# Seven block products for two FFN weight chunks in place of eight, with the sums of the blocks made on GpSimd

## The chip, the cores and the metric

The kernel runs on one core of a Trainium2 chip. The metric is the device time of one execution in microseconds. Before the change three runs gave 2638.39, 2638.54 and 2638.65 us; the median is 2638.54 us. The engines are named as in the profile: PE is TensorE (its weight loads are PEld), DVE is VectorE, ACT is ScalarE, POOL is GpSimd, SP is the queue from which the weight loads are issued.

## The reference, cut to what matters

The model is two layers of a first block and two layers of a second block, on 256 tokens of width 1024. Each layer has an FFN, a mixer and a second FFN, so there are eight FFNs in all:

```python
def swiglu(h, w_gate, w_up, w_down):                 # first block
    return (jax.nn.silu(h @ w_gate) * (h @ w_up)) @ w_down

def swiglu_ffn(h, w_in, w_out):                      # second block
    gate, up = jnp.split(h @ w_in, 2, axis=-1)
    return (jax.nn.silu(gate) * up) @ w_out
# h: 256 x 1024, gate and up: 1024 x 2816 each, down: 2816 x 1024, all float32
```

The change touches the products `h @ w_gate` and `h @ w_up` alone; the mixers and the down product compute what they did.

## The kernel before, in words

**Three products for one.** Every float32 operand is split into a high part, rounded to the type that PE multiplies (`F32R`), and a low part, the rest. `three` (L522 to L524) issues high by high, high by low and low by high into one sum in PSUM. So each weight tile that lands in `ring` (128x1024) is first copied by ACT into `wh` (`high`, L547), and then `wl = ring - wh` is made by DVE or POOL (`low`, L555). Both buffers have four slots; a slot of `wh` is free for the next tile when PE has begun the tile behind it (`used`), and a slot of `ring` when the low part has been made.

**An FFN.** The 2816 columns of gate and of up are cut into 11 chunks of 256. One chunk is four tiles, each with two blocks of 128 rows of 256 gate and 256 up columns, 512 side by side. The activations (`xh`, `xl`, turned so that the width lies on the partitions) are the stationary operand: for each of 8 row blocks and each of 2 groups of 128 tokens (`q`) PE runs three matmuls of 512 columns. A chunk is 48 of them, a tile 12. Chunk 0 goes once through its tiles for each `q`; the others take both `q` in one pass. The sums lie in two banks of PSUM (`GU_BANKS`), ACT applies `Silu` to the gate half (L1436), DVE multiplies with the up half (`gated`, L2023), PE turns the result (four transposes, `turn`, L725), ACT and DVE split it (`turned`, L1441 and L2029). The down product reads 22 more tiles.

**What sets the order.** Each engine's instructions are written out in one fixed order; engines wait for each other with counting semaphores, and nothing is reordered. In the FFNs DVE makes all low parts and POOL none but for a few tiles at their edges; in the mixers POOL makes nearly all of them. SP issues the loads of all tiles in order, each as two transfers of 256 KB, and waits before each for the low part of the tile four before it.

The functions that the diff touches:

Of the kernel before, what the change touches and what calls it, by code (L numbers as in the profile page):

```python
# [13 lines left out]

# [59 lines left out]
assert T1 % SLOTS == 0 and T2 % SLOTS == 0  # L74
# [59 lines left out]
class Tiles:  # L134


    def __init__(self, quads, k=0, widths=None):
        self.quads, self.k, self.it, self.widths = quads, k, 0, widths or {}

    def number(self, i=0):  # L140
        return (self.quads + self.it) * SLOTS + self.k + i

    def slot(self, i=0):
        return (self.k + i) % SLOTS

# [24 lines left out]
def program(nc, a, out, plan):  # L170
# [4 lines left out]
    with ExitStack() as ctx:  # L175
# [16 lines left out]
        wh = sb("wh", [SLOTS, SLOT], F32R)  # L192
        wl = sb("wl", [SLOTS, SLOT], F32R)
# [22 lines left out]
        cmask = masks[:, 0:S]  # L216
        W = sb("W", [WIDE])
# [74 lines left out]
        rows = view(D)  # L292
# [2396 lines left out]
```

## Time and profile before

| what | value |
|---|---|
| median of three runs | 2638.54 us |
| span of the profiled execution | 2636.4 us |
| around the span (difference of the two) | 2.1 us |
| PE busy | 2616.3 us, 99% of the span |
| DVE busy | 1497.4 us, 57% |
| ACT busy | 1435.8 us, 54% |
| POOL busy | 851.6 us, 32% |
| memory traffic | mean 170 GB/s |

The profiled execution's own time is its span and the 2.1 us beside it, so it agrees with the median. Matmuls are pipelined and each is shown longer than its distance to the next, so the busy time of PE says that it never pauses and not how fast it is: its pace is read from the starts in the timeline. POOL is busy in the mixers and idle in the FFNs. An engine's record of an instruction runs from its start to its end; a time in it in which the instruction could not yet read its operands counts as busy.

### The profile page before, as it was taken

What the parts mean: (1) busy time and instruction counts of PE and PEld (TensorE: products, weight loads), DVE (VectorE), ACT (ScalarE), POOL (GpSimd) and SP (SyncE); (2) the same over time, 40 slices, a digit from 0 to 9 for tenths busy, and PEclk for the clock granted to TensorE, in tenths of its full rate; (3) what the DMA queues carried; (4) which work ended last, traced back from release to release, by engine and by line L of the source; (5) the groups of instructions that cost most, each with busy time, mean ns of one, the idle gap of its engine ahead of it and who ended that gap; (6) DMA issues with size and microseconds to landing.
All of it is one profiled execution on the core that took longest, in us unless ns stands there. A gap on an engine that the chain in (4) does not pass through costs nothing.

```text
span 2636.4 us, 45280 instructions
## 1 busy us (share of the span) xinstructions
PE 2616.3 (99%) x16746; PEld 2280.3 (86%) x16746; DVE 1497.4 (57%) x2457; ACT 1435.8 (54%) x2122; POOL 851.6 (32%) x443
## 2 busy tenths in 40 slices
PE   9999999999999999999999999999999999999999
PEld 8888998888888998888889999988888899999887
DVE  5553645545543745545556787355455567873654
ACT  5546665445445655445445645664455557456643
POOL 0007672000017675000008755810000086558100
PEclk9999999999999999999999999999999999999999
DMA  7555546655655546556557742566565587425664
GB/s 226 184 182 177 146 155 188 187 189 180 189 176 175 152 153 198 184 184 194 187 164 184 170 88 82 170 190 187 180 198 186 153 195 166 84 79 184 191 184 144
DMA packets 351973, 447.17 MB, mean 170 GB/s; under 512 B 32446, under 2 KB 241344, under 8 KB 351776
## 3 DMA queue, kind: packets, MB, share of 16 engines
q1 hardware_dynamic: 350032, 442.80, 56.8%
q8 instruction: 133, 2.18, 0.3%
q10 hardware_dynamic: 816, 1.21, 0.1%
q0 software_dynamic: 928, 0.45, 0.1%
q14 instruction: 64, 0.52, 0.1%
HBM read 443.31 MB, written 1.05 MB: 169 GB/s over the span
## 4 chain that ended last, share of the span: by engine, by line
PE 95%; ACT 3%; DVE 2%; issue 0%; POOL 0%; DVEq 0%; ACTq 0%; POOLq 0%
PE PS L522 29%; PE PS L524 29%; PE PS L523 28%; PE PS L725 1%; PE PS L1110 1%; PE PS L1183 1%; PE PS L691 1%; PE PS L1173 1%; PE PS L913 1%; DVE PS L2303 1%; PE PS L960 0%; ACT xh L1320 0%; ACT wh L547 0%; PE PS L826 0%; PE PS L1207 0%
## 5 line engine op out<-in xcount | busy, mean ns | idle before, releaser
L547 ACT ACTIVATE wh<-ring 128x1024 fp32r<-128x1024 f32 (+2 forms) x840 | 883.4, 1055 | 879.9 <-PE PS L522 857.0
L555 POOL TENSOR_TENSOR wl<-ring,wh 128x1024 fp32r<-128x1024 f32 (+2 forms) x332 | 786.1, 2384 | 1589.6 <-ACT wh L547 1589.1
L555 DVE TENSOR_TENSOR wl<-ring,wh 128x1024 fp32r<-128x1024 f32 x508 | 621.4, 1225 | 612.7 <-ACT wh L547 612.4
L522 PE MATMUL PS<-wh,xh 128*128 128x512 f32 (+2 forms) x1760 | 692.3, 393 | 1.0 <-POOL wl L555 1.0
L524 PE MATMUL PS<-wh,xl 128*128 128x512 f32 (+2 forms) x1760 | 682.5, 388 | 0.0
L523 PE MATMUL PS<-wl,xh 128*128 128x512 f32 (+2 forms) x1760 | 681.3, 387 | 0.0
L522 PE MATMUL PS<-xh,wh 128*128 128x256 f32 x1536 | 444.8, 290 | 0.1
L524 PE MATMUL PS<-xh,wl 128*128 128x256 f32 x1536 | 434.4, 283 | 0.0
L523 PE MATMUL PS<-xl,wh 128*128 128x256 f32 x1536 | 434.3, 283 | 0.0
L524 PEld LDWEIGHTS PS<-wh,xl 128*128 128x128 f32 x1760 | 330.5, 188 | 68.4
L522 PEld LDWEIGHTS PS<-wh,xh 128*128 128x128 f32 x1760 | 330.7, 188 | 68.0 <-issue 2.7
L523 PEld LDWEIGHTS PS<-wl,xh 128*128 128x128 f32 x1760 | 331.0, 188 | 63.6
L522 PEld LDWEIGHTS PS<-xh,wh 128*128 128x128 f32 x1536 | 294.1, 191 | 8.4 <-issue 3.4
L523 PEld LDWEIGHTS PS<-xl,wh 128*128 128x128 f32 x1536 | 294.4, 192 | 2.5 <-issue 2.4
L524 PEld LDWEIGHTS PS<-xh,wl 128*128 128x128 f32 x1536 | 294.3, 192 | 0.0
L522 PE MATMUL PS<-wh,hh 128*128 128x512 f32 x704 | 275.2, 391 | 0.0
L524 PE MATMUL PS<-wh,hl 128*128 128x512 f32 x704 | 274.1, 389 | 0.0
L523 PE MATMUL PS<-wl,hh 128*128 128x512 f32 x704 | 273.9, 389 | 0.0
L2303 DVE SCALAR_TENSOR_TENSOR PS<-W,cols,PS 128x256 f32<-128x256 f32 x464 | 186.8, 479 | 0.0
L524 PEld LDWEIGHTS PS<-wh,hl 128*128 128x128 f32 x704 | 132.1, 188 | 27.6
L523 PEld LDWEIGHTS PS<-wl,hh 128*128 128x128 f32 x704 | 132.2, 188 | 27.1
L522 PEld LDWEIGHTS PS<-wh,hh 128*128 128x128 f32 x704 | 132.2, 188 | 26.9
(319 smaller groups left out, 2439.0 us busy)
## 6 DMA issues: line engine op xcount, KB each, us to landing
ring<-in_ffn_w_in_dram SPq DMA_DIRECT2D x352, 256.0 KB, 3.0
ring<-in_mix_w_in_dram SPq DMA_DIRECT2D x256, 256.0 KB, 3.9
ring<-in_ffn_w_gate_dram SPq DMA_DIRECT2D x176, 256.0 KB, 2.9
ring<-in_ffn_w_up_dram SPq DMA_DIRECT2D x176, 256.0 KB, 3.1
ring<-in_ffn_w_down_dram SPq DMA_DIRECT2D x176, 256.0 KB, 2.8
ring<-in_w_in_dram SPq DMA_DIRECT2D x176, 256.0 KB, 3.0
ring<-in_ffn_w_out_dram SPq DMA_DIRECT2D x176, 256.0 KB, 2.8
ring<-in_w_branch_dram SPq DMA_DIRECT2D x32, 256.0 KB, 2.9
```

The lines of the kernel that those rows point to most:

```text
L522: first_ = mm(o, w[0], x[0], start=start, stop=False, skip_group_check=True)
L523: mm(o, w[0], x[1], start=False, stop=False, skip_group_check=True)
L524: return first_, mm(o, w[1], x[0], start=False, stop=stop, skip_group_check=True)
L547: act_(dst, src, ACT.Copy).then_inc(hi_ready, 1)
L555: (engine or v_).tensor_tensor(dst, src, part_views(t, wh)[0], ALU.subtract).then_inc(lo[t.slot()], 1)
L691: ins = nc.tensor.transpose(xt_bank(s, q, k), src[:, q, k * P:(k + 1) * P], ident[:])
L725: ins = nc.tensor.transpose(bank(4 + c % 2, o, o + P), act2[:, c % 2, q, j * P:(j + 1) * P], ident[:])
L913: ins = mm(bank((6 if j == 0 else 4) + half, o, o + nk), heads[r, qb, q * P:(q + 1) * P], heads[r, kb, 0:nk], start=True, stop=True)
L1110: ins = mm(PS[r, 3 + 2 * c, h * HD:(h + 1) * HD], src[c][r, h, :], ident[r, r], start=True, stop=True)
L1173: ins = mm(o, alc[c][r, h, :], lower(Tc[c][r, h, :], l), start=True, stop=True)
L1183: ins = mm(PS[r, 2 + 2 * c, S + h * 32:S + (h + 1) * 32], Uc[c][r, h, :], m1n[c][r, h, :], start=True, stop=True)
L2303: ins = v_.scalar_tensor_tensor(conv[:, b, :] if tap == TAPS - 1 else part, src, w, part, ALU.mult, ALU.add)
```

## The change

Three of the pairs of neighbouring chunks, (3, 4), (6, 7) and (9, 10), are multiplied as 2 by 2 block matrices. The blocks of the left side are the activations cut into front and back half of the width and into the two token groups; the blocks of the right side, `b11`, `b12`, `b21`, `b22`, are 512 rows of one chunk (front or back half of the width, first or second chunk). Seven products M1 to M7 of 4 row blocks each are formed, in place of eight, and the four results are sums of them (Winograd's form of Strassen's algorithm). A product is 12 matmuls of 512 columns and a pair 84, against 96.

- **Loads.** The blocks of a pair land in four buffers of 128x2048 (1 MB each, as two transfers of 512 KB), each loaded again once the product that reads it is done; `b12` waits for M7, `b21` for M2 and for the sum T4. The other five chunks and the down tiles still pass through `ring`. The 28 transfers of `load_params2` move from POOL's queue to SP's.
- **Sums of weights.** POOL makes for each pair T1 = b12 - b11, T2 = b22 - T1, T3 = b22 - b12 and T4 = b21 - T2, each 128x2048. For each FFN it makes once the sums of the activations, S0 (`xh + xl`, 128x2048) and S1 to S4 (128x4x128).
- **High and low parts.** ACT makes the high parts of all seven right sides, 128x2048 each, into both planes of one slot of `wp` (`wh` and `wl` of before as one buffer). DVE makes the low parts of M1, M5 and M3 whole (128x2048), those of M6 in two halves, and half of those of M7, M2 and M4; POOL makes the other halves of these three. The low parts mostly overwrite their source, so that those of M1 and M5 wait for T1 and T2.
- **Sums of products.** ACT copies three of the results out of PSUM, DVE adds three times (128x512).

```diff
+PAIRS = ((3, 4), (6, 7), (9, 10))
+PLAIN_AT = {0: 0, 1: 4, 2: 8, 5: 21, 8: 34}
+PAIR_AT = (12, 25, 38)
+SUM_OF = {"M1": 0, "M5": 1, "M6": 2, "M3": 4, "M7": 5, "M2": 6, "M4": 8}
+SUM_BANKS = {"M1": 6, "M6": 6, "M7": 6, "M4": 6, "M5": 7, "M3": 7, "M2": 3}
+RAW_OF = {"M1": "b11", "M5": "t1", "M6": "t2", "M3": "b22", "M7": "t3", "M2": "b21", "M4": "t4"}
...
+        raw = {n: view(BLOCK) for n in ("b11", "b12", "b21", "b22", "t1", "t2")}
+        low_of = {n: lows[:, i * BLOCK:(i + 1) * BLOCK] for i, n in enumerate(raw)}
+        raw["t3"], low_of["t3"] = raw["b12"], low_of["b12"]
...
+                for i, (name, product) in enumerate((("b11", "M1"), ("b22", "M3"), ("b12", "M7"), ("b21", "M2"))):
...
+                        sp.wait_ge(track_[0].sem, track_[0].at(f"{tag_}.{product}.{p_}", lay_))
+                        if name == "b21":
+                            sp.wait_ge(track_[3].sem, track_[3].at(f"{tag_}.T4.{p_}", lay_))
+                    load_block(sp, p, name, gate, up)
...
+            return (engine or v_).tensor_tensor(dst, src, highs, ALU.subtract)
...
+                product("M1", x_part(0, 0), True)
...
+                product("M5", sum_part(1, 1), True)
+                turn(PAIRS[p][0] - 1)
...
+                product("M6", sum_part(0, 0))
...
+                product("M3", sum_part(1, 0))
...
+                product("M7", sum_part(0, 1))
+                product("M2", x_part(4, 0), True)
...
+                product("M4", x_part(4, 1))
...
+            plain(1, (0,))
+            plain(2, (1,))
+            for p, (c, d) in enumerate(PAIRS):
+                two_chunks(p)
+                if p < 2:
+                    plain(d + 1, (d, c))
...
+                low_behind("M6", 0)
+                low_behind("M6", 1)
                 gated(c - 1)
-                low(e, t, 3 if c == 1 else 2)
+                low_whole(p, "M3", "T3")
                 turned(c - 1)
-                chunk(c)
-                if c < CHUNKS:
-                    low(e, t, 2)
+                low_shared(p, "M7")
+                low_behind("M2", 0)
+                summed(p, bank(7), bank(7), u2s, "M3", "u2s", "c12")
+                low_shared(p, "M4")
+                t.k += PAIR_SLOTS
+                gated_of(d, 0, bank(7, CHUNK, 2 * CHUNK))
+                summed(p, m5s, bank(6), m5s, "M7", "m5s", "c22")
+                low(e, t, 1)
+                gated_of(d, 1, m5s[:, CHUNK:2 * CHUNK])
+                summed(p, bank(3), bank(3), m1s, "M2", "m1s", "c11")
+                low(e, t, 1)
+                gated_of(c, 0, bank(3, CHUNK, 2 * CHUNK))
+                low(e, t, 1)
+                gated_of(c, 1, bank(6, CHUNK, 2 * CHUNK))
+                low(e, t, 1)
+                turned(d)
+                if p < 2:
+                    low_whole(p + 1, "M1", "T1")
...
+                turned(c)
+                if p < 2:
+                    low_whole(p + 1, "M5", "T2")
...
+            did(p_.tensor_tensor(sq, xh, xl, ALU.add), "S0")
...
+            for p in range(3):
...
+                did(p_.tensor_tensor(raw["t1"], raw["b12"], raw["b11"], ALU.subtract), f"T1.{p}")
+                own(f"T1.{p}")
+                e.wait_ge(blocks_in["b22"], landed_)
+                did(p_.tensor_tensor(raw["t2"], raw["b22"], raw["t1"], ALU.subtract), f"T2.{p}")
+                own(f"T2.{p}")
+                did(p_.tensor_tensor(raw["t3"], raw["b22"], raw["b12"], ALU.subtract), f"T3.{p}")
+                e.wait_ge(blocks_in["b21"], landed_)
+                if p == 0:
+                    e.wait_ge(ff[2].sem, ff[2].at(f"{tag}.sl1"))
+                else:
+                    e.wait_ge(ff[0].sem, ff[0].at(f"{tag}.M4.{p - 1}"))
+                did(p_.tensor_tensor(raw["t4"], raw["b21"], raw["t2"], ALU.subtract), f"T4.{p}")
+                own(f"T3.{p}")
+                low_sum(e, t, "M7", p_, 1).then_inc(lo[t.slot(SUM_OF["M7"])], 1)
+                low_sum(e, t, "M2", p_, 1).then_inc(lo[t.slot(SUM_OF["M2"] + 1)], 1)
+                own(f"T4.{p}")
+                low_sum(e, t, "M4", p_, 1).then_inc(lo[t.slot(SUM_OF["M4"])], 1)
```

The order of POOL's instructions, from the setup of the masks on. Before, the first mixer's low parts (L555) come right behind it:

```order
L2630 AFFINE_SELECT masks<-masks 128x128
L555 TENSOR_TENSOR wl<-ring,wh 128x1024 x4
L555 TENSOR_TENSOR wl<-ring,wh 128x912 x4
L555 TENSOR_TENSOR wl<-ring,wh 128x1024 x4
L555 TENSOR_TENSOR wl<-ring,wh 128x512 x4
```

After, the first FFN stands between: S0 to S4, and then for each pair T1 to T4 and three halves of low parts (`W` holds the weight blocks, `sum_lows` the same memory as the place of the low parts). The first pair is shown; the rows from L2915 on come three times.

```order
L2901 TENSOR_TENSOR sq<-xh,xl 128x2048
L2903 TENSOR_TENSOR sq<-sq 128x4x128
L2905 TENSOR_TENSOR sq<-sq 128x4x128
L2907 TENSOR_TENSOR sq<-sq 128x4x128
L2909 TENSOR_TENSOR sq<-sq 128x4x128
L2915 TENSOR_TENSOR W<-W 128x2048
L2918 TENSOR_TENSOR W<-W 128x2048
L2920 TENSOR_TENSOR W<-W 128x2048
L2926 TENSOR_TENSOR sq<-W 128x2048
L685 TENSOR_TENSOR sum_lows<-W,wp 128x1024
L685 TENSOR_TENSOR wp<-W,wp 128x1024
L685 TENSOR_TENSOR sum_low_in_squares<-sq,wp 128x1024
```

So POOL gets 26 instructions in each FFN, in which it had none but at the edges; every one reads two operands from SBUF.

The order of DVE's instructions around the change of chunk, in the first FFN before. Four low parts (L555), two `gated` (L2023) and one `turned` (L2029) are a chunk:

```order
L2029 TENSOR_TENSOR hl<-PS,hh 128x512
L555 TENSOR_TENSOR wl<-ring,wh 128x1024 x2
L2023 SCALAR_TENSOR_TENSOR act<-PS,rs,act 128x256 x2
L555 TENSOR_TENSOR wl<-ring,wh 128x1024 x2
L2029 TENSOR_TENSOR hl<-PS,hh 128x512
L555 TENSOR_TENSOR wl<-ring,wh 128x1024 x2
L2023 SCALAR_TENSOR_TENSOR act<-PS,rs,act 128x256 x2
L555 TENSOR_TENSOR wl<-ring,wh 128x1024 x2
L2029 TENSOR_TENSOR hl<-PS,hh 128x512
```

After, beside the plain chunk 5, which PE multiplies between the first pair and the second. L645 is the low part of a plain tile, L2261 is `gated`, L2289 a sum of products, L2267 is `turned`, L685 the low parts of the next pair's M1 and M5 (`W` in the second row is M5's copy with M7's bank added, `rstd` in the third holds a copy of M1):

```order
L645 TENSOR_TENSOR wp<-ring,wp 128x1024
L2261 SCALAR_TENSOR_TENSOR act<-W,rs,act 128x256
L2289 TENSOR_TENSOR PS<-PS,rstd 128x512
L645 TENSOR_TENSOR wp<-ring,wp 128x1024
L2261 SCALAR_TENSOR_TENSOR act<-PS,rs,act 128x256
L645 TENSOR_TENSOR wp<-ring,wp 128x1024
L2261 SCALAR_TENSOR_TENSOR act<-PS,rs,act 128x256
L645 TENSOR_TENSOR wp<-ring,wp 128x1024
L2267 TENSOR_TENSOR hl<-PS,hh 128x512
L685 TENSOR_TENSOR sum_lows<-W,wp 128x2048
L2267 TENSOR_TENSOR hl<-PS,hh 128x512
L685 TENSOR_TENSOR sum_lows<-W,wp 128x2048
```

The low parts of tiles stand one by one between the results of the pair before, and two whole low parts follow them. By what they wait for, POOL's T1 to T4 of the next pair belong to the same stretch.

## Rows read from the trace of the kernel before

**Rows 1.** The page: busy time of each engine, and the chain that ended last.
```profile
PE 2616.3 (99%) x16746; PEld 2280.3 (86%) x16746; DVE 1497.4 (57%) x2457; ACT 1435.8 (54%) x2122; POOL 851.6 (32%) x443
...
PE 95%; ACT 3%; DVE 2%; issue 0%; POOL 0%; DVEq 0%; ACTq 0%; POOLq 0%
```
**Rows 2.** Busy time by window, nine chunks of one FFN (columns named in its line).
```profile
core 0: us, PE busy (x) PEld busy (x) DVE busy (x) ACT busy (x) POOL busy (x), PEclk, DMA share, GB/s
25.00:149.00 124.00, 124.00 (x570) 102.62 (x569) 72.61 (x89) 62.03 (x79) 0.00 (x0) 1.00 0.61 191
```
**Rows 3.** Timeline of PE in the first FFN: start us, length us, engine, line, instruction.
```profile
10.16 0.48 PE L522 MATMUL PS<-wh,xh 128*128 128x512 f32 x1
...
24.88 0.60 PE L725 MATMUL PS<-ident,act 128*128 128x128 f32 x4
...
36.25 0.60 PE L725 MATMUL PS<-ident,act 128*128 128x128 f32 x4
...
60.81 0.39 PE L522 MATMUL PS<-wh,xh 128*128 128x512 f32 x1
...
62.85 0.39 PE L522 MATMUL PS<-wh,xh 128*128 128x512 f32 x1
```
**Rows 4.** Groups by line and shape: busy us, mean ns, then idle time before them.
```profile
L555 POOL TENSOR_TENSOR wl<-ring,wh 128x1024 fp32r<-128x1024 f32 x316 | 758.9, 2417 | 1572.6 <-ACT wh L547 1572.1
L555 POOL TENSOR_TENSOR wl<-ring,wh 128x512 fp32r<-128x512 f32 x8 | 10.2, 1294 | 6.3 <-ACT wh L547 6.3
L555 DVE TENSOR_TENSOR wl<-ring,wh 128x1024 fp32r<-128x1024 f32 x508 | 621.4, 1225 | 612.7 <-ACT wh L547 612.4
L547 ACT ACTIVATE wh<-ring 128x1024 fp32r<-128x1024 f32 x824 | 870.9, 1060 | 871.2 <-PE PS L522 848.3 <-DMA ring<-in_mix_w_in_dram 15.9 <-DMA ring<-in_w_in_dram 2.4
L1441 ACT ACTIVATE hh<-PS 128x512 fp32r<-128x512 f32 x88 | 51.1, 581 | 0.0
L2023 DVE SCALAR_TENSOR_TENSOR act<-PS,rs,act 128x256 f32<-128x256 f32 x176 | 84.2, 483 | 15.4 <-ACT act L1436 15.4
L2029 DVE TENSOR_TENSOR hl<-PS,hh 128x512 fp32r<-128x512 f32 x88 | 60.1, 683 | 0.0
```
**Rows 5.** Timeline of POOL in the first mixer.
```profile
311.34 2.39 POOL L555 TENSOR_TENSOR wl<-ring,wh 128x1024 fp32r<-128x1024 f32 x1 [0.48 <-ACT wh L547]
316.31 2.49 POOL L555 TENSOR_TENSOR wl<-ring,wh 128x1024 fp32r<-128x1024 f32 x1 [2.58 <-ACT wh L547]
319.17 2.43 POOL L555 TENSOR_TENSOR wl<-ring,wh 128x1024 fp32r<-128x1024 f32 x1 [0.37 <-ACT wh L547]
...
374.25 8.05 POOL L555 TENSOR_TENSOR wl<-ring,wh 128x1024 fp32r<-128x1024 f32 x3 [2.52 <-ACT wh L547]
```
**Rows 6.** Timeline of DVE beside rows 5.
```profile
308.28 1.22 DVE L2168 TENSOR_REDUCE W<-W 128x4 f32<-128x1024 f32 x1
...
314.37 0.42 DVE L2073 TENSOR_TENSOR W<-W,masks 128x256 f32<-128x256 f32 x1
...
316.57 2.79 DVE L2182 TENSOR_TENSOR W<-W 128x512 f32<-128x512 f32 x1
...
324.08 0.68 DVE L1932 TENSOR_TENSOR ol<-W,oh 128x512 fp32r<-128x512 f32 x1
...
376.31 3.71 DVE L1932 TENSOR_TENSOR ol<-W,oh 128x512 fp32r<-128x512 f32 x2
```
**Rows 7.** Timeline of DVE in a mixer of the second block.
```profile
1522.51 2.43 DVE L2303 SCALAR_TENSOR_TENSOR PS<-W,cols,PS 128x256 f32<-128x256 f32 x6
...
1527.59 2.00 DVE L2480 TENSOR_TENSOR W<-masks,W 128x256 f32<-128x256 f32 x1
```
**Rows 8.** Timeline of POOL beside rows 7.
```profile
1519.68 4.74 POOL L555 TENSOR_TENSOR wl<-ring,wh 128x1024 fp32r<-128x1024 f32 x2 [5.62 <-ACT wh L547]
...
1526.82 2.48 POOL L555 TENSOR_TENSOR wl<-ring,wh 128x1024 fp32r<-128x1024 f32 x1 [1.01 <-ACT wh L547]
```
**Rows 9.** The page: loads, their size and median us from issue to landing.
```profile
ring<-in_ffn_w_gate_dram SPq DMA_DIRECT2D x176, 256.0 KB, 2.9
```
**Rows 10.** Timeline of SP in the first FFN: the two transfers of a tile issued.
```profile
36.64 0.37 SPq L358 DMA_DIRECT2D ring<-in_ffn_w_gate_dram  x1
37.10 0.42 SPq L358 DMA_DIRECT2D ring<-in_ffn_w_up_dram  x1
```
**Rows 11.** Busy time by window, the first 30 us (columns as in rows 2).
```profile
0.00:30.00 30.00, 28.12 (x134) 24.12 (x135) 16.80 (x41) 20.82 (x39) 1.52 (x9) 1.00 0.82 261
```

More of the change, by code:

```diff
@@ L15 @@
+import itertools
 import math
@@ L290, in view @@
             return W[:, at:at + width]
-        rows = view(D)
+        rows = post
+        off[0] = 14656
         srow = view(P)
@@ L370, in kmajor, with ffn_number @@
             return w2d.rearrange("(k p) n -> p k n", p=P)
[L372 to L388 removed]
+        def ffn_number(s):
+            return 2 * (s // 3) + s % 3 // 2
@@ new lines, in between @@
+                    def between(last=lay == LAYERS - 1 and half == 1):
+                        if last:
+                            load_params2(sp)
+                    load_ffn(sp, t, first["ffn"], f"f{half}", lay, kmajor(a["ffn_w_gate"][lay, half]),
+                             kmajor(a["ffn_w_up"][lay, half]), a["ffn_w_down"][lay, half],
+                             (first["mix"], lay) if half == 1 else None, before, between)
+                    before = (first["ffn"], f"f{half}", lay, 2)
@@ L508, in program @@
         qd = view(512).rearrange("p (h n) -> p h n", h=4)
+        assert off[0] <= 13824, off[0]
+        off[0] = 13824
+        for c in range(QT):
+            DU["U", c] = view(512).rearrange("p (h n) -> p h n", h=4)
         wT, st = DU["T", 0], DU["T", 1]
@@ L1451, in act_ffn @@
+            silu(0)
+            high(e, t, 3)
+            turned(0)
+            chunk(1)
+            high(e, t, 2)
+            silu(1)
+            high(e, t, 1)
+            turned(1)
+            hi(0, "M1")
+            sums_high()
+            hi(0, "M5")
+            hi(0, "M6")
+            chunk(2)
+            for p, (c, d) in enumerate(PAIRS):
+                two_chunks(p, c, d)
+                for c_ in (c, d, d + 1):
+                    chunk(c_)
             tables(LN_EXP)
@@ L2039, in dve_ffn @@
+            gated(0)
+            low(e, t, 3)
+            turned(0)
+            chunk(1)
+            low(e, t, 2)
+            gated(1)
+            low(e, t, 1)
+            turned(1)
+            low_whole(0, "M1", "T1")
+            sums_low()
+            low_whole(0, "M5", "T2")
+            chunk(2)
+            for p, (c, d) in enumerate(PAIRS):
+                two_chunks(p, c, d)
+                for c_ in (c, d, d + 1):
+                    chunk(c_)
             low(e, t, 8)
```

410 lines of the change are left out of this document (297 added, 113 removed).

## The prediction

> **What bounds the kernel now.** I read first the busy times and the chain of waits: PE is busy 99% of the span, and 95% of the chain that ended last is PE [rows 1]. Then the windows: in 124 us of the first FFN PE never pauses, DVE is busy 72.61 us, ACT 62.03, POOL 0.00, and the granted clock is 1.00, the 2.4 GHz level [rows 2]. Then PE's timeline for its pace: from 60.81 to 62.85 nine matmuls of 512 columns start, 0.227 us each, so a tile of 12 takes 2.72 us; from one turn to the next (24.88 to 36.25) a chunk takes 11.37 us, that is 48 matmuls in 10.88 and 0.49 for the turn; chunk 0 takes 24.88 - 10.16 less one tile, 12.0 us [rows 3]. So an FFN's gate and up products take 12.0 + 10 x 11.37 = 125.7 us, paced by PE alone, and what PE is spared is time gained as long as the others keep up. Last I looked in the timeline of the mixers, the only places where POOL and DVE work together, at what each does to the other: that decides this case.
>
> **The term that gains.** A pair needs 84 matmuls instead of 96. With 3 pairs in each of 8 FFNs that is 288 matmuls fewer, 288 x 0.227 = 65.3 us. The turns stay.
>
> **What POOL and DVE cost each other.** In rows 5 and 6 DVE's L2182 (512 elements, both inputs in `W`) starts at 316.57, while POOL runs from 316.31 to 318.80; it ends at 319.36, 0.56 after POOL's end, and takes 2.79 us. L1932 with the same 512 elements, and with the same kinds of operands as a low part, takes 0.68 when POOL is idle. POOL's next low part, recorded from 319.17, ends at 321.60, 2.24 after DVE's end. At 376.31 two of L1932 take 3.71 us, while three POOL low parts from 374.25 take 8.05 in place of 3 x 2.39 = 7.17: POOL (to 376.64), DVE, POOL, DVE, POOL, in turn. L2480 (256 elements) ends at 1529.59, 0.29 after POOL's end at 1529.30, and takes 2.00; L2073 with as many, beside an idle POOL, takes 0.42 [rows 6 to 8]. DVE instructions with one input in SBUF are not held: six of L2303, which read `W` and PSUM, take 0.41 us each under POOL's two from 1519.68, and the reduction at 308.28 takes its 1.22 [rows 6 to 8]. So a DVE instruction with two SBUF inputs and a POOL instruction exclude each other for their whole length and take turns.
>
> The Trainium skill says the same of the cause (page "SBUF — State Buffer", section "SBUF: two separate sides"): VectorE and GpSimd share a pair of ports, held by whoever starts first for the whole instruction, and VectorE needs it for two inputs in SBUF. The trace agrees with its 0.56 and 0.29 us, and this rule speaks against this change, since it makes no exception for the low parts, which in the trace never meet POOL.
>
> In the FFNs before, nothing of this costs anything, as POOL is idle there. After, POOL has 26 instructions in every FFN, and all low parts of DVE (ring or `W`, and `wp`) have two SBUF inputs.
>
> **Prices.** POOL, 1024 elements: 2.39 alone [rows 5], 2.25 when it waited for DVE (its start is then hidden). From 512 elements at 1.29 [rows 4] the slope is 1.10 us for 512, so 2048 cost 2.39 + 2.20 = 4.6 alone, 4.45 after a wait; no row shows it, the bounds are 4.45 and 2 x 2.39 = 4.8, and I take 4.6. DVE, 1024: 1.22 alone, 1.07 after a wait (0.56 for 512 doubled, less 0.05); 2048: 2.3 and 2.13. ACT: 1.06 for 1024, 0.58 for 512 [rows 4], so 2.0 for 2048. `gated` 0.48, `turned` and a sum from PSUM 0.68 each. A block of 1 MB: 256 KB land in 2.9 us [rows 9] and the memory gave 261 GB/s at best [rows 11], 4 us for a block; with the start of a transfer I take 5, bounds 4 and 7.
>
> **One pair and the chunk beside it.** PE needs 11 x 2.72 + 3 x 0.49 = 31.4 us. The shared access is needed for POOL's T1 to T4, 4 x 4.45, and three halves, 3 x 2.25: 24.6. DVE needs it for three whole low parts 6.4, five halves and four plain tiles 9.6, and one `gated` from SBUF 0.3: 16.3. The sum is 40.9 us, 9.5 more than PE needs. Laid out in turns by the orders of both engines, T1 begins 5 us after M7 of the pair before (b12 has landed). Then DVE's low part of the first plain tile, T2, one `gated`, T3, second tile, T4, third tile follow each other without a gap: 4 x 4.45 + 3 x 1.07 + 0.3 = 21.3 us, in which PE gets two tiles and two turns, 6.4 us of work. The fourth tile, M1, M5, M6 and M3 are then DVE's alone (1.2 + 2.3 + 2.3 + 2.4 + 2.3), with 3.5 us between them for `turned`, `gated` and ACT's high part of M3, which waits for M5's start: 14.0. M7, M2 and M4 need one POOL half and one DVE half each, 3 x 3.4 = 10.2, with 1.1 before them; then 1.1 until T1. Together 21.3 + 14.0 + 1.1 + 10.2 + 1.1 = 47.7 us from T1 to T1. The engines are bound by the shared access for 41 of these and by chains through it for the rest, not by PE.
>
> **The first pair.** S0 begins some 6 us after chunk 0, when the activations' low parts are whole. S0 4.6, S1 to S4 4 x 1.3, and five low parts between them reach to 21; T1, T2, T3 with low parts of tiles 9, 10 and 11 between, 4.4 x 3 + 3.2, to 37.4. `turned`, M1's low part, the two low parts of the activations' sums (T4 waits for them) and M5's bring 45; T4 comes before M6's halves, 52; M3, and M7, M2, M4 with their shares, end at 65; M4 itself ends at 68. PE alone would end there at 12.0 + 8 x 2.72 + 2 x 0.49 + 7 x 2.72 + 0.49 = 54.3.
>
> **Sum.** Gate and up of an FFN: 68 + 2 x 47.7 + 1 (the last `gated` in front of the down product's second half) = 164.4 us, against 125.7: 38.7 more. Eight times that is 310. The profiled execution's time is its span 2636.4 and 2.1 around it, 2638.5, equal to the median; 2638.5 + 310 = 2949, and I forecast 2950. What I cost at nothing: the 28 transfers moved to SP's queue, 0.46 us from one issue to the next [rows 10], some 13 in all, which stand before chunk 5's loads of one FFN, that have 40 us; ACT's extra copies, since ACT has 7 x 2.0 + 4 x 1.06 + 3 x 0.58 + some 4 of results in 47.7 us; the bytes, which are the same as before. If ACT's cover goes, the 2 us of a high part show in M7, 48 us in all, which the range holds.
>
> **Bounds.** If the turns packed without any gap, an FFN would need the access for 9.8 (S0 to S4) + 3 x 24.6 + 16 x 1.07 + 2.1 + 3 x 12.0 = 139 us between 6 us after its start and 2.7 before its end: 147.5, 21.8 more than before, 174 in all, 2813. At the other end POOL at 4.8 instead of 4.45 adds 12 x 0.35 = 4.2 an FFN, and blocks that land in 7 us add 2 in each of two periods: 66 in all, 3015.
>
> **Rivals.**
> *They do not exclude each other here.* The low parts of DVE in FFNs never met POOL, so that it is by kinship with L1932 that I hold them back. Then POOL's 4 x 4.6 + 3 x 2.39 = 25.6 fits under PE's 31.4, DVE needs 25 or so, and the tightest chain, M6's start to M7's low part (0.58 + 2.0 + 2.39 = 5.0) fits under two products, 5.44. PE stays the bound: 2638.5 - 65.3 = 2573, up to 2600 with chains that miss. All overlaps in rows 5 to 8 speak against it. 4%. This is the only way to be faster.
> *Tight packing.* DVE gets ahead by its three tiles in stock, and gaps close: 2813 to 2870. For it speaks that four wl and wh slots are filled when T1 comes; against it that DVE's order puts results between the tiles. 16%.
> *PE's clock falls.* My layout gives PE pauses of 3 to 5 us in each stretch of T1 to T4, where before the longest stretch shown runs without one at 1.00 [rows 2]. If the clock fell to the 1.2 GHz level there and was half until the pause was over, tiles one and two stay hidden under the sums, but the third tile and the start of M1, some 2.7 us of work, would take 2.7 more in each of 24 stretches: 65 us, 3015. No row shows the clock after a pause. 20%.
> The Trainium skill ("TensorE: Matmul & The Clock Gate", part 1, "What's actually happening") has full speed as something that activity grants and idling takes away, between just these two levels; no run here shows it yet.
> *The forecast itself*, 2870 to 3000: 60%.
>
> A change within 0.2%, 5 us, could not be told from none. Faster by more: 4%. Within: 1%. Slower: 95%. The range that holds 8 in 10 reaches from 2830 to 3050.
>
> **What would show it.** PE has 16458 matmuls and its share falls to near 90%. In the chain of waits DVE and POOL have large shares in place of PE's 95%. POOL is busy 690 us more and what it waits, near 1600. The mean of a low part of a plain tile on DVE rises from 1.225 us to 2 or 3, with 5 to 6 for those that wait for a T, each ending 1.07 after POOL's instruction. A window over a middle pair and its chunk takes 47 us with PE busy 35. If the DVE rows stay at 1.2 beside a busy POOL, the whole sum is wrong, and the time is below 2600. If they are long but the kernel is far under 2813, my prices are; if windows show a clock under 1.00, the third rival adds.

## The result and the profile after

The changed kernel takes 2954.7 us, the median of four runs (2949.0 to 2957.9); the kernel before took 2638.5 beside it. The ratio is 1.120, with a 95% interval of 1.118 to 1.121: 316 us slower. The profiled execution took 2955.2 us, its span is 2953.5.

The page after: busy times, granted clock in 40 slices, and the chain that ended last, which answer to [rows 1].
```profile
span 2953.5 us, 42833 instructions
PE 2680.4 (91%) x16458; PEld 2275.9 (77%) x16458; DVE 2071.6 (70%) x2545; ACT 1608.2 (54%) x2234; POOL 1708.2 (58%) x623
PEclk9999999999999999999999999998989999999989
PE 60%; DVE 21%; issue 7%; ACT 6%; DMA 3%; POOL 2%; SPq 1%; POOLq 0%; DVEq 0%; ACTq 0%
```
PE runs 288 matmuls fewer and is no longer always busy. DVE is busy 574 us more than before, although it has only 88 instructions more, and its share of the chain has gone from 2% to 21%.

The groups by line and shape after, which answer to [rows 4]: busy us, mean ns, idle time before them.
```profile
L645 DVE TENSOR_TENSOR wp<-ring,wp 128x1024 fp32r<-128x1024 f32 x316 | 638.2, 2028 | 262.2 <-ACT wp L637 262.2
L645 POOL TENSOR_TENSOR wp<-ring,wp 128x1024 fp32r<-128x1024 f32 x316 | 758.4, 2416 | 718.7 <-ACT wp L637 718.3
L685 DVE TENSOR_TENSOR sum_lows<-W,wp 128x2048 fp32r<-128x2048 f32 x72 | 296.8, 4122 | 11.5 <-ACT wp L673 4.5 <-POOL W L2918 3.9 <-POOL W L2915 3.1
L685 DVE TENSOR_TENSOR wp<-W,wp 128x1024 fp32r<-128x1024 f32 x72 | 152.1, 2138 | 31.2 <-ACT wp L671 31.1
L2918 POOL TENSOR_TENSOR W<-W 128x2048 f32<-128x2048 f32 x24 | 132.1, 5503 | 1.9
```
The same low part of a plain tile, 1.225 us in [rows 4], now takes 2.03 in the mean. POOL's low parts in the mixers are as they were (2.42).

Where it happens: POOL and then DVE in the stretch of T1 to T4 of the second pair, in the first FFN (start us, length us).
```profile
84.16 4.62 POOL L2915 TENSOR_TENSOR W<-W 128x2048 f32<-128x2048 f32 x1 [3.15 <-DMA W<-in_ffn_w_up_dram]
88.85 5.46 POOL L2918 TENSOR_TENSOR W<-W 128x2048 f32<-128x2048 f32 x1
94.39 5.46 POOL L2920 TENSOR_TENSOR W<-W 128x2048 f32<-128x2048 f32 x1
99.79 6.63 POOL L2926 TENSOR_TENSOR sq<-W 128x2048 f32<-128x2048 f32 x1
```
```profile
84.58 5.28 DVE L645 TENSOR_TENSOR wp<-ring,wp 128x1024 fp32r<-128x1024 f32 x1
90.17 5.22 DVE L645 TENSOR_TENSOR wp<-ring,wp 128x1024 fp32r<-128x1024 f32 x1
95.92 6.08 DVE L685 TENSOR_TENSOR sum_lows<-W,wp 128x2048 fp32r<-128x2048 f32 x1
102.52 6.05 DVE L685 TENSOR_TENSOR sum_lows<-W,wp 128x2048 fp32r<-128x2048 f32 x1
```
Read the ends. T1 ends at 88.78, DVE's tile 1.08 later, at 89.86. T2 is recorded from 88.85, ends at 94.31, 4.45 after the tile; the next tile ends 1.08 after T2. So it goes through all four: one at a time, in turn.

PE in the same place, M1 and the start of M5.
```profile
98.08 0.39 PE L615 MATMUL PS<-wp,xl 128*128 128x512 f32 x1
102.05 0.51 PE L613 MATMUL PS<-wp,xh 128*128 128x512 f32 x1 [3.58 <-DVE sum_lows L685]
...
103.54 0.63 PE L614 MATMUL PS<-sum_lows,xh 128*128 128x512 f32 x1
103.97 0.63 PE L615 MATMUL PS<-wp,xl 128*128 128x512 f32 x1
...
108.62 0.50 PE L613 MATMUL PS<-wp,sums_first 128*128 128x512 f32 x1 [1.96 <-DVE sum_lows L685]
```
PE has nothing to do from 98.3 to 102.05 and starts M1 as DVE's low part ends (102.00). From the third on its matmuls start 0.43 us apart instead of 0.227: the clock has fallen to the 1.2 GHz level.

Windows of the same FFN: from the second pair's T1 to the third's; its two parts; and all gate and up products. Columns as in [rows 2].
```profile
84.16:129.17 45.01, 35.53 (x141) 26.73 (x140) 42.67 (x35) 22.27 (x24) 32.18 (x7) 0.92 0.43 133
84.16:106.50 22.34, 16.86 (x69) 12.71 (x67) 22.34 (x9) 9.35 (x11) 22.10 (x4) 0.92 0.38 121
106.50:129.17 22.67, 18.67 (x73) 14.02 (x73) 20.33 (x27) 12.92 (x13) 10.08 (x3) 0.92 0.47 146
10.20:175.40 165.20, 132.95 (x543) 101.94 (x542) 148.71 (x116) 90.49 (x114) 109.77 (x26) 0.94 0.46 150
```
In the first part DVE and POOL are both recorded as busy throughout, which two engines that take turns show, since the record counts the wait.

The loss is in the FFNs alone. From first turn to last an FFN took 113.6 us before (all eight within 113.61 to 113.65) and takes 151.2 to 154.5 after. Eight times the mean difference of 39.2 is 314 of the 316 us.

### The profile page after: what moved, and what is told of

It reads as the page before. It is cut to its first block, busy times and chain, and to the rows that moved or that the text cites. A ratio compares the mean times of both kernels' runs of the same rounds, so it can differ in the third digit from the quotient of the medians.

```text
span 2953.5 us, 42833 instructions
## 1 busy us (share of the span) xinstructions
PE 2680.4 (91%) x16458; PEld 2275.9 (77%) x16458; DVE 2071.6 (70%) x2545; ACT 1608.2 (54%) x2234; POOL 1708.2 (58%) x623
## 4 chain that ended last, share of the span: by engine, by line
PE 60%; DVE 21%; issue 7%; ACT 6%; DMA 3%; POOL 2%; SPq 1%; POOLq 0%; DVEq 0%; ACTq 0%
PE PS L613 18%; PE PS L615 17%; PE PS L614 17%; DVE wp L645 8%; DVE sum_lows L685 7%; ACT wp L673 2%; DVE wp L685 2%; DVE act L2261 1%; DMA ring<-in_ffn_w_up_dram 1%; ACT wp L637 1%; PE PS L869 1%; DMA ring<-in_ffn_w_in_dram 1%; POOL sum_low_in_squares L685 1%; DVE hl L2267 1%; ACT xh L1498 1%
## 5 line engine op out<-in xcount | busy, mean ns | idle before, releaser
L645 POOL TENSOR_TENSOR wp<-ring,wp 128x1024 fp32r<-128x1024 f32 (+2 forms) x332 | 785.6, 2383 | 735.6 <-ACT wp L637 735.2
L637 ACT ACTIVATE wp<-ring 128x1024 fp32r<-128x1024 f32 (+2 forms) x648 | 681.3, 1054 | 638.5 <-PE PS L613 535.7
L645 DVE TENSOR_TENSOR wp<-ring,wp 128x1024 fp32r<-128x1024 f32 x316 | 638.2, 2028 | 262.2 <-ACT wp L637 262.2
L613 PE MATMUL PS<-wp,xh 128*128 128x512 f32 (+2 forms) x1280 | 532.4, 416 | 118.3 <-DVE sum_lows L685 58.7
L615 PE MATMUL PS<-wp,xl 128*128 128x512 f32 (+2 forms) x1280 | 513.1, 401 | 0.0
L613 PE MATMUL PS<-xh,wp 128*128 128x256 f32 x1536 | 445.2, 290 | 0.2 <-POOL wp L645 0.2
L615 PE MATMUL PS<-xh,wp 128*128 128x256 f32 x1536 | 434.6, 283 | 0.0
L614 PE MATMUL PS<-xl,wp 128*128 128x256 f32 x1536 | 434.6, 283 | 0.0
L614 PE MATMUL PS<-wp,xh 128*128 128x512 f32 (+2 forms) x1088 | 428.7, 394 | 0.0
L613 PEld LDWEIGHTS PS<-wp,xh 128*128 128x128 f32 x1280 | 251.9, 197 | 206.4 <-DVE sum_lows L685 68.5
L613 PE MATMUL PS<-wp,hh 128*128 128x512 f32 x896 | 361.9, 404 | 9.0 <-issue 9.0
L685 DVE TENSOR_TENSOR sum_lows<-W,wp 128x2048 fp32r<-128x2048 f32 x96 | 326.2, 3398 | 29.6 <-ACT wp L673 22.6
L614 PE MATMUL PS<-wp,hh 128*128 128x512 f32 x800 | 317.8, 397 | 0.0
L613 PEld LDWEIGHTS PS<-xh,wp 128*128 128x128 f32 x1536 | 294.3, 192 | 8.7 <-issue 3.1
L615 PEld LDWEIGHTS PS<-xh,wp 128*128 128x128 f32 x1536 | 294.5, 192 | 0.0
L614 PEld LDWEIGHTS PS<-wp,xh 128*128 128x128 f32 x1088 | 210.2, 193 | 38.1
L685 POOL TENSOR_TENSOR sum_lows<-W,wp 128x1024 fp32r<-128x1024 f32 x24 | 80.9, 3372 | 213.1 <-ACT wp L673 213.1
```

Source lines behind the costliest of these rows:

```text
L613: first_ = mm(o, w[0], x[0], start=start, stop=False, skip_group_check=True)
L614: mm(o, w[0], x[1], start=False, stop=False, skip_group_check=True)
L615: return first_, mm(o, w[1], x[0], start=False, stop=stop, skip_group_check=True)
L637: act_(dst, src, ACT.Copy).then_inc(hi_ready, 1)
L645: (engine or v_).tensor_tensor(dst, src, part_views(t, wh)[0], ALU.subtract).then_inc(lo[t.slot()], 1)
L685: return (engine or v_).tensor_tensor(dst, src, highs, ALU.subtract)
```

## The experiments

All are compared with the kernel before, whose median was 2638.3 us beside them. The times are medians.

**1. POOL busy but reading nothing.** Each of T1 to T4 becomes three memsets of the same result, so the sums of weights are left out.

```diff
-                did(p_.tensor_tensor(raw["t1"], raw["b12"], raw["b11"], ALU.subtract), f"T1.{p}")
+                did(p_.memset(raw["t1"], 0.0), f"T1a.{p}")
+                own(f"T1a.{p}")
+                did(p_.memset(raw["t1"], 0.0), f"T1b.{p}")
+                own(f"T1b.{p}")
+                did(p_.memset(raw["t1"], 0.0), f"T1.{p}")
```

> Leaves out T1 to T4: each is replaced on POOL by three memsets of the same 128x2048 block, some 5.5 us together, so that POOL is busy as long as before or a little longer but reads nothing from SBUF. Theory (a POOL instruction that reads SBUF and a DVE instruction with two SBUF inputs exclude each other): DVE's low parts are no longer held by the sums, only by the three halves; the mean of a plain tile's low part on DVE falls from 2.03 us to below 1.4, and the kernel to 2600 to 2690 us. Rival one (POOL is simply too slow, and its sums come too late): POOL's time per pair is the same or longer, so 2940 us or more. Rival two (writes exclude DVE as well): the low parts stay long, 2950 to 3050 us.

Measured: 2693.5 us, ratio 1.022 (1.020 to 1.024), clock 0.992. POOL and then DVE in this kernel, from T1 of the second pair on (three memsets for each T):
```profile
71.92 1.81 POOL L2915 MEMSET W<- 128x2048 f32 x1 [1.94 <-DMA W<-in_ffn_w_up_dram]
73.79 1.82 POOL L2917 MEMSET W<- 128x2048 f32 x1
75.66 1.81 POOL L2919 MEMSET W<- 128x2048 f32 x1
```
```profile
71.98 1.21 DVE L645 TENSOR_TENSOR wp<-ring,wp 128x1024 fp32r<-128x1024 f32 x1
73.56 1.23 DVE L645 TENSOR_TENSOR wp<-ring,wp 128x1024 fp32r<-128x1024 f32 x1
78.91 2.29 DVE L685 TENSOR_TENSOR sum_lows<-W,wp 128x2048 fp32r<-128x2048 f32 x1 [1.18 <-ACT wp L673]
```
POOL is as long in its sums as before, and DVE makes its low parts at its own price, 1.22 and 2.29, through all of it. What held the low parts was that POOL read, not that it was busy or late. This takes 261 of the 316 us away. The time is 3.5 us above the expected range, and the mean of a plain tile's low part is 1.48 us, not below 1.4: S0 to S4 and the halves still read.

Other instructions of DVE are held by the memsets. In the same stretch DVE works out angles, once in the whole kernel; DVE and then POOL:
```profile
85.32 1.53 DVE L2544 CAST W<-W 128x2 f32<-128x2 int32 x1
86.89 0.17 DVE L2546 TENSOR_TENSOR W<-W 128x16 f32<-128x16 f32 x1
87.09 1.63 DVE L2547 TENSOR_SCALAR W<-W 128x16 f32<-128x16 f32 x1
```
```profile
85.02 1.81 POOL L2930 MEMSET W<- 128x2048 f32 x1
86.89 1.81 POOL L2932 MEMSET W<- 128x2048 f32 x1
```
The `CAST` and the `TENSOR_SCALAR` have one tensor as input. They end 0.02 and 0.03 us after a memset; in the changed kernel, where POOL is idle at that point, they take 0.16 and 0.17. Three more `TENSOR_SCALAR` behind them are held in the same way (1.75, 1.20 and 1.62 us), some 7 us in all. The `TENSOR_TENSOR` between, with two inputs, is not held.

**2. POOL short and reading nothing.** One memset in place of three.

```diff
-                did(p_.tensor_tensor(raw["t1"], raw["b12"], raw["b11"], ALU.subtract), f"T1.{p}")
+                did(p_.memset(raw["t1"], 0.0), f"T1.{p}")
```

> Leaves out T1 to T4: each is replaced by one memset of the block, some 1.8 us. Theory: PE is nearly the bound again; what is left are S0 to S4 and the three halves, 2590 to 2660 us, and near what the run with three memsets gives. If the sums' length were the cause, this run would be faster than the one with three memsets by 24 x 4 x 3.7 us at most, some hundred us or more.

Measured: 2683.9 us, ratio 1.018 (1.016 to 1.019). The shorter time that POOL is busy is thus worth 10 us. In the profiled executions, which are 13 us apart, 8 us of the difference lie in the first FFN, where the memsets of experiment 1 held DVE's angles, so the length of the sums is worth little by itself. The expected range was missed by 24: what is left, 111 us above the 2573 that PE's matmuls alone would give, has other causes. From one pair's M4 to the next this kernel and that of experiment 1 need 33.7 us, where PE needs 31.4.

**3. Shorter turns.** T1 to T4 as two instructions of 1024 elements each.

```diff
-                did(p_.tensor_tensor(raw["t1"], raw["b12"], raw["b11"], ALU.subtract), f"T1.{p}")
+                p_.tensor_tensor(raw["t1"][:, 0:1024], raw["b12"][:, 0:1024], raw["b11"][:, 0:1024], ALU.subtract)
+                did(p_.tensor_tensor(raw["t1"][:, 1024:2048], raw["b12"][:, 1024:2048], raw["b11"][:, 1024:2048], ALU.subtract), f"T1.{p}")
```

> T1 to T4 are issued as two instructions of 1024 elements each, nothing else changes. Theory (the sum of both engines' shared access sets the period): the sum is the same but for 0.15 us an instruction, so 2930 to 2970 us, the time after the change within 1%. Rival (it is the length of a single hold, 4.6 us, for which DVE's next low part stands): DVE gets in twice as often, PE's tiles come in time, below 2880 us.

Measured: 2915.0 us, ratio 1.105 (1.103 to 1.106), between the two expectations, both of which missed. A tile's low part takes 1.76 us in the mean instead of 2.03, since it waits behind half a sum. So the length of a turn is worth 40 us; the rest of the loss is still there with turns of half the length.

**4. The three halves made by DVE.** POOL keeps T1 to T4.

```diff
-                low_shared(p, "M7")
+                low_whole(p, "M7", "T3")
                 low_behind("M2", 0)
+                low_behind("M2", 1)
...
-                low_shared(p, "M4")
+                low_whole(p, "M4", "T4")
```

> The three halves of low parts that POOL makes for each pair (M7, M2, M4) are made by DVE; T1 to T4 stay on POOL. Theory: the shared access is needed 3 x 2.25 us less by POOL and 3 x 1.07 more by DVE, 3.5 us less a pair, in a stretch in which both take turns and PE waits for both: 24 x 3.5 = 85 us less, some 2870 us (2840 to 2900). Rival (there the period is set by PE at half clock, or by ACT's high parts): no change, 2945 to 2960 us.

Measured: 2929.3 us, ratio 1.111 (1.109 to 1.113); 25 us gained where 85 were expected, which is between the two expectations. The changed kernel's own rows say why. There M7, M2 and M4 start at 120.50, 123.91 and 127.36, 3.4 us apart as forecast (POOL's 2.26 and DVE's 1.1), but PE needs 2.72 for each, so halves cost 0.7 us a product and not the whole of their turns. Three such steps in 24 pairs could give at most about 50. In this kernel the three start at 117.81, 120.53 and 123.70, and the step from M4 to M4 is mostly 43.8 us in place of 45.3.

**5. The sums on DVE, POOL idle in the FFNs.** All of T1 to T4, S0 to S4 and the halves move to DVE, the sums between its low parts.

```diff
+HOOKS = {('plain', 1): ['S0'], ('plain', 2): ['S1', 'S3', 'S2', 'S4', 'sums', ('T1', 0), ('T2', 0)], ('inM6', 0): [('T3', 0)], ('inM3', 0): [('T4', 0)], ('P2', 0): [('T1', 1)], ...
```

> All of POOL's 26 instructions of each FFN (S0 to S4, T1 to T4, the halves) are made by DVE, between the low parts of the plain tiles; same three pairs, same result. Theory: nothing is held any more, every DVE instruction takes its time alone (1.22 and 2.3 us), and DVE's own work is the bound: for a pair and its chunk 4 x 2.3 for the sums, 7 x 2.3 and 4 x 1.22 for low parts, 7 for results, 37.2 us, against 45 now and 31.4 for PE. 2720 to 2830 us: much faster than after the change although DVE has more to do, and still slower than before. Rival (DVE's load, not the holding, costs the time after the change): DVE has 14 us more a pair, so slower than 2955 us.

Measured: 2756.7 us, ratio 1.045 (1.043 to 1.046): 198 us faster than the change, by giving DVE all of POOL's work. Its groups on DVE: tiles, low parts of products, and T1 to T3:
```profile
L655 DVE TENSOR_TENSOR wp<-ring,wp 128x1024 fp32r<-128x1024 f32 x316 | 383.8, 1221 | 249.4 <-ACT wp L647 249.3
L695 DVE TENSOR_TENSOR sum_lows<-W,wp 128x2048 fp32r<-128x2048 f32 x96 | 218.5, 2283 | 13.5 <-ACT wp L683 13.5
L2343 DVE TENSOR_TENSOR W<-W 128x2048 f32<-128x2048 f32 x72 | 164.5, 2284 | 2.5 <-DMA W<-in_ffn_w_up_dram 1.1 <-DMA W<-in_ffn_w_in_dram 0.6
```
A sum costs DVE 2.28 us where POOL needs 4.6 and holds DVE that long. With POOL idle DVE's tile is back at 1.22. It is still slower than before, since DVE's own work for a pair and its chunk is over the 31.4 us that PE needs: 11 x 2.28 for sums and low parts, 4 x 1.22 for tiles, and for results 6 x 0.48, 3 x 0.68 and 3 x 0.69, together 37 us. The step from M4 to M4 is 37.2 us in most of its FFNs, which is this sum: here DVE sets the pace.

**6. One pair in each FFN, all on DVE.** Chunks 6 and 7 alone; T1 to T4 are spread over chunks 3 to 5.

```diff
-PAIRS = ((3, 4), (6, 7), (9, 10))
+PAIRS = ((6, 7),)
+HOOKS = {('plain', 1): ['S0'], ('plain', 2): ['S1', 'S3', 'S2', 'S4'], ('plain', 3): ['sums', ('T1', 0)], ('plain', 4): [('T2', 0), ('T3', 0)], ('plain', 5): [('T4', 0)]}
```

> Only chunks 6 and 7 of each FFN are multiplied with seven products, all sums and low parts on DVE, and spread over chunks 1 to 5; POOL idle in the FFNs. Theory: PE stays the bound and DVE's 24 us more an FFN lie in its 51 us of idle time: 8 x 12 matmuls x 0.227 = 21.8 us less than before, less some waits in the pair: 2617 to 2630 us. Rival (a pair has chains of its own, high part, low part, product, that cost PE more than 2.7 us): 2638 us or more.

Measured: 2640.4 us, ratio 1.0010 (1.0001 to 1.0019), outside the range and where the rival had it. Five FFNs were shorter than before by 1.1 to 1.7 us and two by 0.3 and 0.2, but the fourth took 124.15 us in place of 113.63. SP in that FFN, from the first small transfer to the next tile's load, and what PE waited for there:
```profile
1026.83 0.41 SPq L363 DMA_DIRECT2D post<-in_ffn_norm_pre_dram  x1
...
1035.40 0.39 SPq L414 DMA_DIRECT2D ring<-in_ffn_w_gate_dram  x1
```
```profile
PEld PS L623 <- DVE wp L655: 6.1, 1, 6.1
```
The 28 small transfers of `load_params2` hold SP for 8.6 us in front of a plain tile's loads. Experiment 9 tests whether that is the cause.

**7. Two pairs.** As 6, with chunks (4, 5) and (9, 10).

```diff
+PAIRS = ((4, 5), (9, 10))
```

> Chunks (4, 5) and (9, 10) of each FFN with seven products, all on DVE, POOL idle in the FFNs. Theory: PE would need 43.5 us less than before; DVE is needed for 62 of 65 us up to the end of the first pair and 50 of 54 in the second stretch, so that some of it comes back as waits: 2600 to 2650 us. If DVE's load costs more than its share says: above 2650 us.

Measured: 2665.2 us, ratio 1.010 (1.009 to 1.012), above the expected 2600 to 2650. FFNs take 118.4 to 119.6 from first turn to last, the first one 126.2. Two pairs seem to be too much for DVE already: the turns' weight loads wait for `gated` for 51 us in all. That it is DVE's load is argued from this wait.

**8. Unused sums on POOL in the kernel before.** Nothing of the change is in it; POOL gets 35 subtractions of 1024 elements and four of 512 in each of the first four FFNs, each of one buffer from itself.

```diff
+            big(2)
+            big(4, HALF)
+            for c in (0, 3, 6):
+                e.wait_ge(ff[0].sem, ff[0].at(f"{tag}.gu{c}.1"))
+                big(8)
+                big(2, SLOT)
+                big(1, SLOT, f"ffn{s}.{c}")
```

> The kernel before, unchanged in what it computes, with POOL instructions added that nobody's data depends on, in the four FFNs of the first block alone: after the activations are split 2 of 1024 and 4 of 512 elements, and after chunks 0, 3 and 6 eleven of 1024 each, all with two SBUF inputs. Theory: while POOL runs, DVE gets one low part for each POOL instruction, 2.25 + 1.07 = 3.3 us a tile against PE's 2.72, so some 15 us for each of the four FFNs: 2680 to 2710 us, and DVE's low parts in these FFNs take 2 to 3.3 us. Rival (no exclusion; the change is slow for its own chains): 2638 us, and the low parts stay at 1.22 us.

Measured: 2648.5 us, ratio 1.004 (1.003 to 1.005). DVE's low parts and POOL in the second FFN:
```profile
443.21 5.14 DVE L556 TENSOR_TENSOR wl<-ring,wh 128x1024 fp32r<-128x1024 f32 x2
448.28 0.86 DVE L2024 SCALAR_TENSOR_TENSOR act<-PS,rs,act 128x256 f32<-128x256 f32 x2
449.06 4.96 DVE L556 TENSOR_TENSOR wl<-ring,wh 128x1024 fp32r<-128x1024 f32 x2
```
```profile
444.52 25.42 POOL L2598 TENSOR_TENSOR heads<-heads 128x1024 f32<-128x1024 f32 x9
```
The exclusion is there on the very instruction of which no row of before showed it: 2.5 us in place of 1.2. `gated`, which reads PSUM too, keeps its price (0.86 us for two). But PE is not late in three of the four FFNs (113.75 to 113.79 us). POOL and DVE alternate, and one low part and one subtraction together take 2.83 us (nine in 25.42), so that four tiles take 11.3, within the 11.37 us of a chunk. Only the first, where DVE also works out the angles, loses 10; there the `CAST` and three of the `TENSOR_SCALAR` are held too (1.25 to 1.75 us). I had expected 3.3 us a tile; it is 2.83, since these subtractions take POOL 1.91 us alone and 1.75 behind DVE, not 2.25. So this run shows the exclusion and not what it costs in time.

**9. One pair, the small transfers back on POOL's queue.**

```diff
-                    def between(last=lay == LAYERS - 1 and half == 1):
-                        if last:
-                            load_params2(sp)
+                    def between():
+                        pass
...
             e.wait_ge(first["mix"][2].sem, first["mix"][2].at("mc3"))
+            load_params2(e)
```

> One pair per FFN with all sums and low parts on VectorE, as in e6_one_pair, but the 28 small transfers of load_params2 are issued by GpSimd's queue again, behind the last low part of the first mixers as in the kernel before, and not by SP in front of the loads of chunk 4. In e6_one_pair the FFN with these transfers took 124.15 us from first turn to last (before 113.62), the other two that were read 113.3 and 111.9 (before 113.64). Theory (the transfers hold SP's loads back, so PE runs out of tiles): that FFN falls to 112 to 113, and the time from 2640.4 by 11 to 12 us to 2629, range 2624 to 2633, below the kernel before. Rival (the loss of that FFN is the pair's own, there, say by the wait of its blocks for the mixer's buffers): within 3 us of e6_one_pair, 2637 to 2643.

Measured: 2628.8 us (2627.4 to 2631.5), ratio 0.9964 (0.9951 to 0.9978). The fourth FFN takes 111.91 us. This version is 9.5 us (0.4%) faster than the kernel before, with 96 matmuls fewer; these are worth 21.8. Where the other 12 us stayed was not taken apart.

**10. The pauses filled.** The changed kernel with twelve unread matmuls before M1 and before M5 of each pair.

```diff
+            if n in ("M1", "M5"):
+                for _ in range(12):
+                    mm(bank(SUM_BANKS[n]), xh[:, 0, 0:P], hh[:, 0:512], start=True, stop=True)
             low_ready(pe, t, u)
```

> The changed kernel with twelve matmuls of 512 columns more, whose results nobody reads, in front of M1 and of M5 of every pair, ahead of their wait for DVE's low part: 576 in all, 576 x 0.227 = 131 us of PE work put into PE's pauses. In the changed kernel PE paused from 98.3 to 102.05 before M1 and M1's 12 matmuls then took 4.45 us in place of 2.72, at the 1.2 GHz level, and so did M5's from 108.62; the mean granted clock was 0.965. Theory (the lower clock is almost wholly hidden, because M5 waits for DVE's low part, which ends at 108.57 whatever PE does, and the turn behind M5 waits for gated): the clock rises to above 0.98 and the time stays within 8 us of 2955, 2947 to 2963. Rival (the clock is part of the loss, as in my prediction's third rival): M5's 1.7 us in each of 24 stretches come back, 41 us, or both products' 3.4, 82 us: 2873 to 2914. If the time rises by more than 8 us, the pauses are shorter than the matmuls put into them and the run decides nothing on the clock unless the clock stayed low too.

Measured: 2955.1 us (2953.7 to 2962.0), ratio 1.121 (1.119 to 1.123), with the mean clock at 0.986 instead of 0.965. The window 84.16 to 129.17 and PE around M1:
```profile
84.16:129.17 45.01, 37.82 (x165) 28.98 (x164) 42.68 (x33) 22.53 (x25) 32.39 (x7) 1.00 0.44 138
```
```profile
103.56 0.50 PE L613 MATMUL PS<-wp,xh 128*128 128x512 f32 x1 [0.89 <-DVE sum_lows L685]
103.90 0.39 PE L614 MATMUL PS<-sum_lows,xh 128*128 128x512 f32 x1
104.13 0.40 PE L615 MATMUL PS<-wp,xl 128*128 128x512 f32 x1
```
M1 now runs at full speed, and nothing is gained by that: M5 waits for DVE anyway. But the equal time does not show that the lower clock costs nothing, since it is the sum of a gain and a loss. The gain is in M5. In the second pair of the fourth FFN DVE's low part for M5 ends at 1214.95 in the changed kernel; the starts of M5 and M4 there, and then here, where the low part ends at 1220.26:
```profile
1215.01 0.57 PE L613 MATMUL PS<-wp,sums_first 128*128 128x512 f32 x1 [1.95 <-DVE sum_lows L685]
...
1233.01 0.47 PE L613 MATMUL PS<-wp,xh 128*128 128x512 f32 x1 [0.46 <-POOL sum_low_in_squares L685]
```
```profile
1220.32 0.50 PE L613 MATMUL PS<-wp,sums_first 128*128 128x512 f32 x1 [0.88 <-DVE sum_lows L685]
...
1236.96 0.47 PE L613 MATMUL PS<-wp,xh 128*128 128x512 f32 x1 [0.46 <-POOL sum_low_in_squares L685]
```
M4 starts 18.06 us behind the low part at the lower clock and 16.70 at the full one. In eight of the changed kernel's 24 stretches M5 is slow in this way and M4 comes some 1.35 us later, about 11 us in all (an estimate). The loss is in the unread matmuls: in 13 of the 24 stretches here they outlast the pause, M5 starts 2.4 to 3.6 us behind its low part, and in four of these M4 comes 1.1 to 2.4 us later than in the changed kernel. So the lower clock is a consequence of the pauses that adds some 11 of the 316 us, and the run does not give its price more exactly.

## Why the prediction was right

The forecast was 2950 (2870 to 3000 for the mechanism itself); 2954.7 was measured. The mechanism is shown: experiment 1 removes the reads of POOL's sums and keeps their length, and 261 us go; 8 adds reads on POOL and nothing else, and DVE's low parts are held; 5 gives all of the work to DVE, although it was busier than POOL, and gains 198 us.

- **The gain.** 288 matmuls, as said. Since PE mostly waits for DVE in the FFNs, the 65.3 us show in no shorter time there; how much of them is hidden was not measured.
- **Prices.** POOL's sum alone 4.55 to 4.62 (4.6), after a wait 4.45 (4.45), DVE's tile behind it 1.08 (1.07); its 5.2 to 5.3 us lie in the forecast 5 to 6. POOL's half and DVE's half took 3.4 together, as said.
- **One pair and its chunk.** 45.0 us against 47.7. The stretch of T1 to T4 took 22.3 (21.3), the rest 22.7 (26.4). The order within it was another: two tiles and then M1's and M5's low parts stood between the sums, and not three tiles, because DVE had got ahead by the tiles in stock, as the rival of tight packing had it. With that, less was left for the second part. The rival named the right fact and the wrong sum: the alternation was as dense, and the products behind it set the rest.
- **The first pair.** M4 ended at 84.1, 73.9 after the start of chunk 0, against 68. T1 came at 37.77, 27.6 after that start, against 21. The term that was mis-sized is the one in front of T1. S0 began 9.0 us after the start of chunk 0 and not 6. S0 to S4 with DVE's low parts between them took 13.5, less than the 15 forecast. POOL then waited 5.03 us for b12, which I had not counted for the first pair. DVE (the window ends at 24.5) and then POOL:
```profile
20.92 3.97 DVE L645 TENSOR_TENSOR wp<-ring,wp 128x1024 fp32r<-128x1024 f32 x1 [2.74 <-ACT wp L637]
```
```profile
23.88 2.16 POOL L2903 TENSOR_TENSOR sq<-sq 128x512 f32<-128x512 f32 x1
...
37.77 4.55 POOL L2915 TENSOR_TENSOR W<-W 128x2048 f32<-128x2048 f32 x1 [5.03 <-DMA W<-in_ffn_w_up_dram]
```
The 2.16 us recorded for S1 hold its wait: DVE's low part ends at 24.89, S1 at 26.04, 1.15 later, so that the price of 1.3 was right.
- **The sum.** 73.9 and the two steps from M4 to M4, 46.1 and 44.7, are 164.7 us for the gate and up products, against 164.4. That these agree to 0.3 us is luck: +5.9 for the first pair, -4.6 for the two others, -1.0 for the end. Eight FFNs at +39 give the rest.
- **The clock.** The third rival had its fact, the 1.2 GHz level behind PE's pauses, and not its price: the rows beside experiment 10 give some 11 us (an estimate) where it gave 65, since most of the slow matmuls lie in front of a wait for DVE. The forecast had left these 11 us out, which is luck of the same kind.
- **What is not held.** The prediction says that DVE instructions with one input in SBUF are not held. For its two examples that is so, for all such instructions it is not: experiment 1 shows a `CAST` and four `TENSOR_SCALAR` held even by memsets, and the trace before has a `TENSOR_SCALAR` of two elements that ends 0.03 us after POOL's low part (302.86 to 305.25) and takes 0.23 where POOL is idle:
```profile
304.57 0.71 DVE L2180 TENSOR_SCALAR W<-W,lam 128x2 f32<-128x2 f32 x1
```
It changed nothing in the sum, as such instructions are rare in the FFNs.
- **Costed at nothing.** The small transfers on SP were hidden in the changed kernel (its fourth FFN takes 152.4 us, the others 151.2 to 154.5), as forecast, but that they fit was not given: in experiment 6 the same transfers, 8.6 us of SP's time in front of another chunk, cost 11.6 us (2640.4 to 2628.8).
- **What the profile was to show.** Twice I named it wrongly. POOL has 2% of the chain and not a large share: the chain goes through DVE's instruction, whose record holds the wait for POOL. And POOL is busy 1708 us, not near 1600, for the same reason.

How the 381.5 us between 2573.2 (PE's matmuls alone) and the changed kernel divide is only partly settled. 261 go with POOL's reads in T1 to T4 and what follows from them, the slower clock too, and 10 with its time for them. Of the other 111 the halves may have some 47 (an estimate): in the first FFN of experiment 1 PE pauses 0.76, 0.57 and 0.64 us before M7, M2 and M4 of a pair, 24 times 1.97. The rest was not taken apart: S0 to S4, results on DVE and waits for blocks are among it.

## What to carry to other kernels

Before work is moved to an idle engine, look in the trace for a place where it already runs beside the busy one, and compare ends there: if one ends a fixed time after the other, they share an access, and each instruction moved can cost the busy engine the whole length of the slower one's. Look at each kind of instruction by itself, since not all are held by the same. A busy record can hold a wait, so take prices from end to end. Here POOL's 4.6 us for a sum was dearer than DVE's own 2.3. A saving on the bounding engine is worth only as much as the next engine has room for: of three, two and one pair only one paid, by 0.4%, and it did so once a queue that had seemed free was cleared.

## What the runs showed of the hardware that was not expected

- A memset on POOL does not hold DVE's low parts, which have two SBUF inputs: they take 1.22 us beside POOL's memsets and 5.2 beside its subtractions. It does hold DVE's `CAST` and `TENSOR_SCALAR` (1.53 and 1.63 us in place of 0.16 and 0.17). The Trainium skill has both kinds ("SBUF — State Buffer", "SBUF: two separate sides"): against a VectorE operation with two SBUF inputs only an operation of GpSimd that reads SBUF counts, and against one in a 2-port performance mode any. Both measurements fit it; in which mode the `CAST` and the `TENSOR_SCALAR` ran, no run shows.
- A subtraction of 128x1024 of a buffer from itself took POOL 1.91 us alone (experiment 8); a low part of the same size, with two buffers and a rounded result, takes 2.39 [rows 5]. Which of the two differences makes it was not tried.
- After a pause of 3.6 us PE's matmuls of 512 columns started 0.43 us apart, from 102.69 to 105.68, and 0.23 again from 106.04. With the pause cut to 0.89 us by unread matmuls they started 0.23 apart from the second on.
